# First feed-forward units taken block by block in block 1, and weight splits moved ahead of other ScalarE work

## The reference, cut to what matters

```python
def _swiglu(t, w_gate, w_up, w_down):
    return (jax.nn.silu(t @ w_gate) * (t @ w_up)) @ w_down

for l in range(DEPTH):                      # block 1
    f = _swiglu(_rmsnorm(h, ffn1_pre_g[l]), ffn1_w_gate[l], ffn1_w_up[l], ffn1_w_down[l])
    h = h + 0.5 * _rmsnorm(f, ffn1_post_g[l])
    ...
    h = h + _rmsnorm(merged @ w_out[l], mix_post_g[l])
    f = _swiglu(_rmsnorm(h, ffn2_pre_g[l]), ffn2_w_gate[l], ffn2_w_up[l], ffn2_w_down[l])
    h = h + 0.5 * _rmsnorm(f, ffn2_post_g[l])
...
# block 2: x = layer_norm(ALPHA * x + 0.5 * swiglu(x)), then the gating unit:
z = gelu(x @ w_in + b_in)
u, v = jnp.split(z, 2, axis=-1)
v = layer_norm(v, ln_g, ln_b)
mixed = jnp.einsum('gts,bcsgd->bctgd', w, v) + b_sp
return (u * mixed) @ w_out
# ... and behind the scan: ((y + bonus) * g) @ w_o
```

## Time and profile before

| | us |
|---|---|
| median of three executions | 2973.78 |
| lowest, highest | 2970.81, 2977.2 |
| the profiled execution | 2970.68 |
| its span in the trace | 2968.9 |
| PE busy | 2856.4 |
| DVE busy | 1723.5 |
| ACT busy | 1385.3 |

### The profile page before, as it was taken

How to read it: one execution, slowest core, us unless ns; L and a number is a source line. 1 busy time by engine, 2 the same in 40 slices (tenths; PEclk the granted TensorE clock), 3 DMA queues, 4 the chain that set the end, 5 groups by cost and what they waited for, 6 DMA issues and landing times.

```text
span 2968.9 us, 53772 instructions
## 1 busy us (share of the span) xinstructions
PE 2856.4 (96%) x23700; PEld 2666.6 (90%) x23700; DVE 1723.5 (58%) x2001; ACT 1385.3 (47%) x1759; POOL 169.5 (6%) x197
## 2 busy tenths in 40 slices
PE   8999999999999999999999999999997999998998
PEld 8999999999999999999989899999987899886887
DVE  6555656546455657455455664554787555575555
ACT  5445555445445645444445444443461344454444
POOL 1000110000000010001000000000011000063000
PEclk9999999999999999999999999999999999998999
DMA  7444444454443434446554455455330255441453
GB/s 265 185 171 144 155 143 186 185 198 173 182 170 143 156 143 185 185 185 229 197 192 165 168 190 194 156 213 199 140 110 18 94 187 190 176 161 44 162 193 128
DMA packets 69730, 494.27 MB, mean 166 GB/s; under 512 B 7853, under 2 KB 9421, under 8 KB 10870
## 3 DMA queue, kind: packets, MB, share of 16 engines
q1 hardware_dynamic: 64224, 465.54, 42.7%
q10 hardware_dynamic: 5274, 25.30, 2.3%
HBM read 489.70 MB, written 1.06 MB: 165 GB/s over the span
## 4 chain that ended last, share of the span: by engine, by line
PE 82%; DVE 7%; ACT 5%; issue 3%; POOL 2%; DMA 0%; DVEq 0%; POOLq 0%; SPq 0%; ACTq 0%
PE front L105 51%; PE acc L105 29%; ACT weights_hi L118 2%; DVE weights_lo L332 2%; POOL conv_gate L3443 1%; POOL conv_out L3446 1%; DVE weights_block_lo L332 0%; ACT b_att_w_by_query L1211 0%; DVE h L704 0%; ACT weights_block_hi L118 0%; ACT act_gate L690 0%; DMA weight_ring<-in_weights 0%; DVE b_att_stats L1190 0%; DVE h L719 0%; POOL b_att_w_by_key L1458 0%
## 5 line engine op out<-in xcount | busy, mean ns | idle before, releaser
L332 DVE TENSOR_TENSOR weights_lo<-weight_ring,weights_hi 128x2048 fp32r<-128x2048 f32 x298 | 684.8, 2303 | 535.0 <-ACT weights_hi L118 534.4
L118 ACT ACTIVATE weights_hi<-weight_ring 128x2048 fp32r<-128x2048 f32 x298 | 566.2, 1907 | 114.1 <-PE acc L105 84.3
L105 PE MATMUL front<-b_x_hi,weights_hi 128*128 128x256 f32 x2128 | 601.4, 283 | 10.1 <-DVE b_x_lo L777 7.2
L105 PE MATMUL front<-b_x_lo,weights_hi 128*128 128x256 f32 x2128 | 597.4, 281 | 0.0
L105 PE MATMUL front<-b_x_hi,weights_lo 128*128 128x256 f32 x2128 | 597.0, 281 | 0.0
L332 DVE TENSOR_TENSOR weights_block_lo<-weight_ring,weights_block_hi 128x2048 fp32r<-128x2048 f32 x137 | 315.5, 2313 | 298.2 <-ACT weights_block_hi L118 298.1
L105 PEld LDWEIGHTS front<-b_x_hi,weights_hi 128*128 128x128 f32 x2128 | 402.8, 189 | 20.0 <-DVE weights_lo L332 9.5
L105 PEld LDWEIGHTS front<-b_x_lo,weights_hi 128*128 128x128 f32 x2128 | 402.7, 189 | 1.8
L105 PEld LDWEIGHTS front<-b_x_hi,weights_lo 128*128 128x128 f32 x2128 | 401.8, 189 | 0.0
L105 PE MATMUL front<-b_x_hi,weights_block_hi 128*128 128x256 f32 x1376 | 389.7, 283 | 2.5 <-DVE b_x_lo L777 2.5
L105 PE MATMUL front<-b_x_lo,weights_block_hi 128*128 128x256 f32 x1376 | 389.3, 283 | 0.0
(11 more groups left out here) (555 smaller groups left out, 5423.6 us busy)
## 6 DMA issues: line engine op xcount, KB each, us to landing
weight_ring<-in_weights SPq DMA_DIRECT2D x440, 1024.0 KB, 4.8
xn<-in_norm_rows ACTq DMA_DIRECT2D x14, 1024.0 KB, 4.9
sgu_bias_row<-in_sgu_rows ACTq DMA_DIRECT2D x1, 2048.0 KB, 10.7
sgu_norm_rows<-in_sgu_rows ACTq DMA_DIRECT2D x1, 2048.0 KB, 9.5
bias_hankel<-bias_scratch ACTq DMA_DIRECT2D x1, 1536.0 KB, 7.9
h<-in_x SPq DMA_DIRECT2D x2, 512.0 KB, 5.7
mem_norm<-in_memory SPq DMA_DIRECT2D x1, 1024.0 KB, 13.3
sgu_w_spatial<-in_sgu_w_spatial ACTq DMA_DIRECT2D x1, 1024.0 KB, 4.8
```

What stands on the lines that cost most here:

```text
L105: return pe.matmul(out, a, b, start=start, stop=stop, skip_group_check=True)
L118: return act.activation(out, in_, ACT.Copy, scale=scale)
L332: dve.tensor_tensor(w.lo, k.ring[:, n % RING, :], w.hi, ALU.subtract) \
```

## The change

Four stage boundaries (w_out to the second feed-forward in both layers, layer 0 to layer 1, block 1 to block 2) now use `pe_ffn_head`. The norm functions are cut into functions of one block, and new ones interleave them: the second norm of block 0 comes before the first norm of block 1, and x of block 0 is made between. PE's dummy matmuls go from 12 + 12 to 8 in block 1's boundaries, and to none at the way to block 2. The norm rows, and seven loads for the gating unit at block 2's start, are issued by ACT behind unit 1 of the feed-forward instead of before it. At block 2's start two places of units are swapped (`TURNED2`), so that both first units lie in slots that block 2 may use. In the gating unit the splits of turns 9 and 10 move ahead of the Squares, and one split moves behind the first turned part; behind the scan one weight split moves between the parts of `gated_y`.

```diff
+def act_add_norm_head(k, act, of, done, scale, norm):
+    act.preload_act_table(ACT.Sqrt)
+    act_add_norm_block(k, act, of, done, scale, 0)
+    act_norm_block(k, act, norm, ("made", of, 0, 1), 0)
+    act_add_norm_block(k, act, of, done, scale, 1)
+    act_x_block(k, act, norm, 0)
+    act_norm_block(k, act, norm, ("made", of, 1, 1), 1)
...
+def dve_add_norm_head(k, dve, of, done, norm):
+    dve.wait_ge(*k.s.at("loaded_rows", of))
+    dve.wait_ge(*k.s.at("acc", done, 0))
+    for i in range(2):
+        dve_gain_half(k, dve, of, 0, i)
+    dve_add_block(k, dve, of, 0)
+    dve_norm_block(k, dve, norm, 0)
+    dve.wait_ge(*k.s.at("acc", done, 1))
+    for i in range(2):
+        dve_gain_half(k, dve, of, 1, i)
+        dve_x_half(k, dve, norm, 0, i)
+    dve_add_block(k, dve, of, 1)
+    dve_norm_block(k, dve, norm, 1)
+    dve_x_block(k, dve, norm, 1)
...
     k.slots = FFN1_SLOTS
-    pe_ffn(k, pe, ("ffn1", l), *ffn_units(1, l), split_mark(("pre1", l)), {} if l else {0: lambda: pe_memory(k, pe)})
+    pe_ffn(k, pe, ("ffn1", l), *ffn_units(1, l), split_mark(("pre1", l)), {} if l else {0: lambda: pe_memory(k, pe)},
+           head=(("pre1", l), k.t, 8) if l else None)
...
-    pe_features(k, pe, ("pre2", l), k.t, in_parts(("pre2", l)), warm=12, midway=("made", ("mixed", l), 1, 0))
-    pe_ffn(k, pe, ("ffn2", l), *ffn_units(2, l), split_mark(("pre2", l)))
+    pe_ffn(k, pe, ("ffn2", l), *ffn_units(2, l), None, head=(("pre2", l), k.t, 8),
+           turned_at=TURNED2 if l else ())
...
+def act_ffn_head(k, act, f, norm, two=False):
+    act_ffn(k, act, f, {1: lambda: act_load_rows(k, act, f, ("made", norm, 1, 1))}, two=two, head=norm)
...
-    pe_features(k, pe, ("in2",), k.h, in_parts(("in2",)), warm=12, made=("ffn2", 1))
-    others_drained(k, pe, "pe", 1)
...
     for l in range(L1):
         act_layer(k, act, l)
+    drained(k, act, "act", 1)
+    act.preload_act_table(ACT.Sqrt)
+    act_add_norm_block(k, act, ("ffn2", 1), ("ffn2", 1), 0.5, 0)
     others_drained(k, act, "act", 1)
+    k.x, k.hid = k.x2, k.hid2
+    act_x_block(k, act, ("in2",), 0)
+    act_add_norm_block(k, act, ("ffn2", 1), ("ffn2", 1), 0.5, 1)
...
     for i in range(16):
-        hi(k, act)
+        if i not in (9, 10):
+            hi(k, act)
         for b in range(NB):
             act_sgu_tile(k, act, 2 * i + b)
         if i in (8, 9):
+            hi(k, act)
             b = i - 8
...
             if n == 0:
                 act.wait_ge(*k.s.at("tile", of, 31))
                 act.wait_ge(*k.s.at("bias_stored"))
-                hi(k, act)
             act.wait_ge(*k.s.at("uv_turned", n))
             copy_act(act, sgu_parts(k, 2 * n).hi, turned_pair(k, n)).then_inc(*k.s.up("x_hi", ("uv", 2 * n), 0))
+            if n == 0:
+                hi(k, act)
...
-            if n == 0:
-                lo(k, dve)
             dve.wait_ge(*k.s.at("x_hi", ("uv", 2 * n), 0))
             x = sgu_parts(k, 2 * n)
             dve.tensor_tensor(x.lo, turned_pair(k, n), x.hi, ALU.subtract).then_inc(*k.s.up("x_lo", ("uv", 2 * n), 0))
+            if n == 0:
+                lo(k, dve)
...
+    for q in range(0, KT, 2):
+        act_high(k, act, ("gated_y",), y, k.out_x, q, ("y_gated", q // 2))
+        if q == 2:
+            hi(k, act)
+    act_units(k, act, 4)
...
+TURNED2 = (("up", 7), ("down", 6))
...
-    pe_ffn(k, pe, ("f2", 0, 0), *ffn2_units(0, 0), split_mark(("in2",)), slots=FFN2_SLOTS)
+    pe_ffn(k, pe, ("f2", 0, 0), *ffn2_units(0, 0), None, head=(("in2",), k.h, 0, ("ffn2", 1)), slots=FFN2_SLOTS)
```

More of the change, by code:

```diff
@@ L667, in act_norm, with dve_norm_block @@
-        act.wait_ge(*k.s.at("sq_sum", of, b))
-        act.activation(stat(k, 5, b), stat(k, 4, b), ACT.Sqrt, scale=1 / D, bias=k.eps(1e-6)) \
-            .then_inc(*k.s.up("std", of, b))
+        act_norm_block(k, act, of, ready(b), b)
+def dve_norm_block(k, dve, of, b):
+    dve.wait_ge(*k.s.at("std", of, b))
+    dve.reciprocal(stat(k, 7, b), stat(k, 5, b)).then_inc(*k.s.up("rstd", of, b))
+    dve.wait_ge(*k.s.at("rstd", of, b))
+    for i in range(2):
+        dve.scalar_tensor_tensor(out=half(k.t[:, b], i), in0=half(k.h[:, b], i), scalar=stat(k, 7, b),
+                                 in1=half(k.rows[:, 1], i), op0=ALU.mult, op1=ALU.mult) \
+            .then_inc(*k.s.up("made", of, b, i))
@@ L672, in dve_norm @@
 def dve_norm(k, dve, of):
     for b in range(NB):
[L674 to L680 removed]
+        dve_norm_block(k, dve, of, b)
@@ L889, with pe_ffn @@
 FF = DFF // 256
-def pe_ffn(k, pe, f, gate, up, down, ready, beside={}, head=None, slots=None, turned_at=None):
+def pe_ffn(k, pe, f, gate, up, down, ready, beside={}, head=None, slots=None, turned_at=()):
     def make(j):
@@ L914, in use @@
     def use(j):
-        k.turned = turned_at == ("down", j)
+        k.turned = ("down", j) in turned_at
         ap = unit(k, pe, *down(j), a=2)
```

192 lines of the change are left out of this document (101 added, 91 removed).

## The result

Seven executions of the changed kernel took 2963.77 us in the median (2954.6 to 2968.93), seven of the kernel before 2975.52 (2970.44 to 2984.21): a ratio of 0.9947, with a 95% interval of 0.9929 to 0.9964. The medians lie 11.8 us apart, 0.4%, and the interval leaves 1 out. The forecast was 2959.9, with a range of 2953 to 2968; 2963.77 lies in the range, and 0.3 above the inner stretch of 2956 to 2963.5 that had the chance of 0.57. The profiled execution took 2958.35 with a span of 2956.5, 12.3 us less than that of before; the sum had been 13.9.

What follows compares the result with a forecast made beforehand. PE, busy 2856.4 of 2968.9 us, was taken as the bound. Gains of 4.2 + 2.0 + 5.1 + 1.5 + 1.1 = 13.9 gave 2956.8 profiled and 2959.9 as median, with a range of 2953 to 2968.

Steps and rivals of the forecast that it cites:

- T: The moment PE is through with the old stage at a boundary; first matmul in block 1 forecast 3.88 us later.
- the new wait: Gating unit: with two waits removed, PE would wait 1.5 us at the next unit; net gain 5.1.
- the first down unit: Gating unit's first down unit: with DVE's split moved behind, PE's 1.73 wait falls to about 0.3, gaining 1.5 us.
- behind the scan: Behind the scan: an earlier weight split shrinks PE's wait of 1.10 to about 0.1, gaining 1.1 us.
- The boundaries: Three stage boundaries in block 1, each with its first unit: gain 1.4 us each, 4.2 to 4.3 for three.
- Into block 2: Way into block 2 with its first unit: 15.1 against 17.1, gain 2.0 us; bounds 0.7 and 3.1.
- The step that failed: Feed-forwards: seven moved loads and two swapped slots cost nothing, since splits end about one unit of matmuls early.
- Clock in the heads: Rival: granted clock falls in the four heads, costing 1.65 us each; 2966.5 us, chance 0.12.
- Stall in the gating unit: Rival: the gating unit's stall only moves, by a longer wait or lower clock; 3 less gain, 2962.9, chance 0.12.
- x of block 1: Rival: x of block 1 is not late in the heads; gain 21.2 at most, 2956 more likely, chance 0.09.
- Gain eaten by delayed splits: Rival: swapped slots or moved loads delay splits in 11-unit loops; within 6 of 2974, chance 0.06.
- Slower: Rival: half clock stays for the whole head, 13 us each, 39 for three; 2998 us, chance 0.04.

Runs made afterwards that it cites:

- v_all: Changed kernel with three further moves of weight splits (block 1's heads, last gate/up turn of its second feed-forwards, gating unit); median 2947.0, ratio to before 0.9904.
- the second group: Changed kernel executed again unchanged, with the kernel before in the same group; medians 2955.94 and 2980.82, ratio 0.9918.
- after_again: Second trace of the changed kernel, nothing altered; median of its six executions 2955.94, ratio to before 0.9918.
- after: First trace of the changed kernel, nothing further altered; this profiled execution took 2958.35 us.

## Why the prediction was right, and where not

**The mechanisms stand.** First matmul at T+3.89 for a forecast of 3.88, unit 1 at T+18.8 for 18.9; the new wait 1.42 for 1.5; the clock at 1.00 in all four heads; 0.28 for about 0.3 at the first down unit; 1.20 for 1.1 behind the scan.

**The boundaries came out close**, 1.5 each for 1.4 with the units behind them counted in (1.74 less 0.14 and 0.09; the sum had 0.15 for both). I had added 2.45 of waits to a head of 12.55. The recorded idle times, 0.57 and 0.97, are shorter than what the waits cost, since a matmul's recorded length reaches into the time of the next. By the starts the first wait cost 0.72 and the last 1.13, and a third hides in the row of eight turned tiles, 1.32 long where block 2's is 1.03: 0.29. Together that is 2.14. The rest of the head's 14.91 is a pace of 0.120 for a matmul instead of 0.118.

**Into block 2** two misses met. The first matmul came at T+2.73 for 2.4; of this the drain, 0.3 in the sum with no row behind it, was 0.41. The head took 12.33 for 12.55. That 2.07 came out near 2.0 is luck in part. The bound of 3.1 for the faster pace was too wide as well: 10.98 for 11.51, applied to 12.55, takes off 0.6, which gives 2.6.

**The step that failed** is a term that the sum put at nothing: "nothing on PE waits for that point, since in a feed-forward a split ends about one unit of matmuls (5.7, half of 11.51) before PE wants it", said of the moved loads and, with "the same lead", of the swapped slots. The lead covers a split that comes late; it does not cover what a split delays. With the slots swapped layer 1 also takes two splits ahead instead of one; this is the end of `ahead=2 - l` (l is the layer) in the full change, here on DVE:

```diff
-    dve_ffn(k, dve, ("ffn2", l), first=0, two=True, ahead=2 - l)
...
+    dve_ffn(k, dve, ("ffn2", l), two=True, head=True)
```

So a third split stands on DVE in front of the glu: 2.28 us of work ahead of the values that PE wants next. It cost 1.07, and v_all took it back without cost. The same wait stood in layer 0 before the change, and could have been read there (PE, before):

```profile
675.36 0.47 PE L105 MATMUL acc<-weights_block_hi,b_hidden_hi 128*128 128x512 f32 x1 [0.91 <-DVE b_hidden_lo L1103]
```

**What was not in the sum at all** is the position of the code. Block 3 won 6 us in the profiled pair and 3 to 16 between any two traces with and without the old count; the scan lost 3.0 in the pair, of which the position explains the longer stalls. In the profiled pair this came to about 3 us of gain, which the first unit (1.5) and the pace of units 337 to 345 (1.7), both chance, ate; that 12.3 stood so near 13.9 is therefore partly luck. In the second group the medians lie 25 us apart instead of 12; block 3 at 85 instead of 76 would fit that, but the executions behind those medians were not traced. Why block 3's stretch is 76 in some executions of the kernel before and 85 in others (in the longer two, PE waited 2.94 instead of 0.87 for GpSimd within it, and the clock was lower) stays open. So does which stretch held the changed kernel's longest executions, 2964.7 to 2968.93 at a mean clock of 0.989 or 0.990; there is no trace of them.

**The rivals.** Clock in the heads: not with 8 dummies, once in six without. Stall in the gating unit: only the 1.42. x of block 1: late, as taken. Gain eaten by delayed splits: yes, but only the 1.07. Slower: no sign.

## What to carry to other kernels

Ask of each split or load that is taken earlier what it now stands in front of, on its own engine, and not only whether it comes in time: three small moves of that kind gave 8 us here by the traces, two thirds of the 12 that the large change gave. Before adding up a change that alters the number of an engine's instructions, look for idle times with the releaser "issue" in stretches of short instructions; they move with the count, anywhere behind the edit, and only a comparison unit by unit (or padding) tells them from the change itself. A recorded idle time in front of a matmul is less than what the wait costs; compare starts. Where executions scatter by 15 us, a sum of 14 is tested by distances within traces, and the medians come last.

## What the runs showed of the hardware

- TensorE's instructions come in packets of 16 KB, 256 instructions. In stretches of short matmuls it stalls for 0.3 to 2.5 us at a spacing of 256; in the scan these stalls sum to 6 to 10 us, in block 3 to 2 to 6. With 194 instructions fewer ahead block 3 took 69 to 70 us instead of 76 to 85.
- A wait of 3.11 to 3.32 lowered the granted clock for the unit behind it in all four traces that have it (0.77 to 0.79), one of 1.42 to 1.44 in none of twelve. Without dummies around eight turned tiles the clock fell in one head of six, with idle times (1.07 and 0.96) that do not set it apart from the other five.
- The table load of 1.28 was followed at once, in the heads too (498.62 to 499.91); no drain of its own was seen.
- The same 48 matmuls took 5.44 us in some units and 5.65 in others, at a granted clock of 1.00 in both (units 257 to 261 in after_again and after).
